# Final norm of the odd tiles on ScalarE and GpSimd instead of VectorE, and one semaphore for five products of the plan

## Chip, cores and metric

One core of one Trainium2 chip. The metric is the device time of one execution in microseconds (us), as a median over runs.

## What is computed

One step of a decoder layer: norm, input projection, convolution group and sparse attention group, output projection, residual, norm, a mixture of 32 gated experts (two per token), residual, and a last norm. Only the end of it matters here:

```python
def rmsnorm(x, g):
    xf = x.astype(jnp.float32)
    y = xf * lax.rsqrt(jnp.mean(xf * xf, axis=-1, keepdims=True) + RMS_EPS)
    return (y * g.astype(jnp.float32)).astype(x.dtype)
# the experts' results, weighted and summed per token, are added to x; then
# y = rmsnorm(x, ln_final), for 1024 prompt rows and 32 sample rows of D_MODEL = 1024
```

## The kernel before

The tokens are 1056 rows: eight tiles of 128 rows and a ninth (tile 8) of 32. All values are float32. The program is written as one stream per engine, with semaphores between them; an engine runs its stream strictly in the order written. `chain(ins)` makes an engine wait for its own instruction `ins`.

The last block of the kernel has two parts that the diff touches.

**The plan** (VectorE from L2312, TensorE from L2278). VectorE works out which expert takes which rows in which round. TensorE supplies five products in this order, each with a semaphore of its own: `counted`, `prefixed`, `experts_turned` (L2287), `table_made` (36 products at L2293), `small_doubled` (L2298). VectorE waits for them at L2326, L2354 (`experts_turned`), L2361 (`prefixed`), L2406 and L2411.

**The experts** follow: 17 rounds, each with one expert on 128 rows and one on up to 64, whose weights stream in through SyncE's queue while TensorE multiplies. GpSimd gathers rows and scatters results to `scratch_y` in device memory.

**The final stage** begins when the last results are in `scratch_y`. Four streams run it, each over the nine tiles in order:

- SyncE, `load_results` (L2229): for every tile two loads of 512 KB (the two experts' rows), into one of three places (YS = 3). The loads of tile t wait until the sums of tile t - 3 are done.
- VectorE, `sum_results`: in step t the two weighted sums of tile t (L2246, one SCALAR_TENSOR_TENSOR per expert), then, of tile t - 1, the reciprocal of the root (L2254) and one SCALAR_TENSOR_TENSOR that multiplies by it and by the gains `final_g` into `final` (L2257). `final` has two places, one for even tiles and one for odd ones; before L2257 of tile q, VectorE waits at L2256 until the store of tile q - 2 has landed (`final_out0`, `final_out1`).
- ScalarE, `result_moments`: Square with a sum over the row (L2265), then the root (L2267). It loads the table of the root first (L2261).
- GpSimd, `store_results`: waits for `final_ready` and issues the store of 512 KB (L2236). Tile 8 is 32 rows. At the end it waits until all stores have landed.

The lines of VectorE and GpSimd that the change replaces:

```python
if q >= 2:
    dve.wait_ge(sem(f"final_out{q % 2}"), 16 * (q // 2))
dve.scalar_tensor_tensor(final[:n, q % 2, :], x_res[:n, q, :], rs9[:n, q:q + 1],
                         final_g[:n, :], ALU.mult, ALU.mult).then_inc(sem("final_ready"), 1)
...
pool.wait_ge(sem("final_ready"), t + 1)
pool.dma_start(dst, final[:rows(t), t % 2, :]).then_inc(sem(f"final_out{t % 2}"), 16)
```

Earlier in the kernel, other lines serve as measures: L849 is GpSimd's addition of a bias to 128x512; L636 and L638 are its copies of 128x256; L542 and L545 are VectorE's taps of the convolution on 128x1024, a TENSOR_SCALAR and then SCALAR_TENSOR_TENSORs; L1679, L1681 and L1690 are ScalarE's Square, Sqrt and Copy in the stage of the second norm.

Of the kernel before, what the change touches and what calls it, by code (L numbers as in the profile page):

```python
# [24 lines left out]
ALU = mybir.AluOpType  # L25
# [113 lines left out]
def build(nc, a):  # L139

    _, const_at, const_small = const_table()
    with ExitStack() as ctx:
# [11 lines left out]
        def sem(name):  # L154

            if name not in semaphores:
                semaphores[name] = nc.alloc_semaphore(name)
            return semaphores[name]
# [2073 lines left out]
        def store_results(pool):  # L2232
            for t in range(TILES):
                pool.wait_ge(sem("final_ready"), t + 1)
                dst = out["out0"][P * t:P * t + P, :] if t < NQ else out["out1"]
                pool.dma_start(dst, final[:rows(t), t % 2, :]).then_inc(sem(f"final_out{t % 2}"), 16)  # L2236
            pool.wait_ge(sem("final_out0"), 16 * 5)
            pool.wait_ge(sem("final_out1"), 16 * 4)

        def sum_results(dve, chain):  # L2240
            for t in range(TILES + 1):
                if t < TILES:
                    n = rows(t)
                    dve.wait_ge(sem(f"y_rows_in{t % YS}"), 32 * (t // YS + 1))
                    for j, w in enumerate((first_w, second_w)):
                        ins = dve.scalar_tensor_tensor(x_res[:n, t, :], y_rows[:n, t % YS, j, :], w[:n, t:t + 1],  # L2246
                                                       x_res[:n, t, :], ALU.mult, ALU.add)
                        if j == 0:
                            chain(ins)
                    ins.then_inc(sem("rows_summed"), 1)  # L2250
                if t >= 1:
                    q, n = t - 1, rows(t - 1)
                    dve.wait_ge(sem("sd9_ready"), q + 1)
                    chain(dve.reciprocal(rs9[:n, q:q + 1], sd9[:n, q:q + 1]))  # L2254
                    if q >= 2:
                        dve.wait_ge(sem(f"final_out{q % 2}"), 16 * (q // 2))  # L2256
                    dve.scalar_tensor_tensor(final[:n, q % 2, :], x_res[:n, q, :], rs9[:n, q:q + 1],  # L2257
                                             final_g[:n, :], ALU.mult, ALU.mult).then_inc(sem("final_ready"), 1)

        def result_moments(act, chain):  # L2260
            chain(act.activation(table9, con("eps")[:, 0:1], ACT.Sqrt))  # L2261
            for t in range(TILES):
# [4 lines left out]
                act.activation(sd9[:n, t:t + 1], ms9[:n, t:t + 1], ACT.Sqrt, bias=con("eps")[:n, 0:1])\  # L2267
                   .then_inc(sem("sd9_ready"), 1)

        with nc.Block() as block:  # L2270
# [7 lines left out]
            def _(pe):  # L2278
                for name in ("upped0", "upped1", "downed0", "downed1", "xg_turned0", "xg_turned1"):
                    pe.sem_inc(sem(name), 1)  # L2280
                pe.matmul(ps[:, 1, 0:E_], con("ones"), counted_to[:, TILES], start=True, stop=True)\
                  .then_inc(sem("counted"), 1)
                pe.matmul(ps[:, 0, 0:288], con("before"), both.rearrange("p t n -> p (t n)"), start=True, stop=False)
                pe.matmul(ps[:, 0, 0:288], con("ones"), counted_to[:, 0:TILES].rearrange("p t n -> p (t n)"),
                          start=False, stop=True).then_inc(sem("prefixed"), 1)
                pe.wait_ge(sem("experts_set"), 1)
                pe.matmul(ps[0:1, 3, 0:COLS + 1], expert_f, ident[:, 0:COLS + 1], start=True, stop=True)\  # L2287
                  .then_inc(sem("experts_turned"), 1)
                for q in range(2 * TILES):
                    n = rows(q % TILES)  # L2290
                    if q % TILES == 0:
                        pe.wait_ge(sem("one_hots"), q // TILES + 1)
                    mm = pe.matmul(ps[:, 2, 0:COLS], one_slot[:n, q, :], one_chunk[:n, q, :],  # L2293
                                   start=(q == 0), stop=(q == 2 * TILES - 1))
                mm.then_inc(sem("table_made"), 1)
                pe.wait_ge(sem("small_table"), 1)
                for h in range(2):
                    mm = pe.matmul(ps[HF * h:HF * h + HF, 7, 0:ROUNDS], ident[:HF, :HF], small_table[:HF, :],  # L2298
                                   start=True, stop=True, tile_position=(0, HF * h))
                mm.then_inc(sem("small_doubled"), 1)  # L2300
                expert_products(pe)
# [11 lines left out]
            def _(dve):  # L2313
                chain = Chain(dve, sem("dve_chain"), count["dve"])

                def each(v):
# [8 lines left out]
                n_large, n_small = n_both[:, 0:E_], n_both[:, E_:2 * E_]  # L2325
                dve.wait_ge(sem("counted"), 1)  # L2326
                dve.tensor_scalar(n_large, ps[:, 1, 0:E_], -0.5, 1.0 / P, ALU.add, ALU.mult)
# [25 lines left out]
                                               ALU.subtract))  # L2353
                dve.wait_ge(sem("experts_turned"), 1)  # L2354
                dve.tensor_copy(row_ints[0:1, 0:2 * ROUNDS + 1], ps[0:1, 3, 0:COLS + 1]).then_inc(sem("plan_ready"), 1)
# [4 lines left out]
                chain(dve.tensor_scalar(shift, shift, float(ROUNDS), float(P), ALU.add, ALU.mult))  # L2360
                dve.wait_ge(sem("prefixed"), 1)  # L2361
                places = ps[:, 0, 0:288].rearrange("p (t n) -> p t n", n=E_)
# [42 lines left out]

                dve.wait_ge(sem("table_made"), 1)  # L2406
                large, small = ps[:, 2, 0:ROUNDS], ps[:, 7, 0:ROUNDS]
                dve.tensor_copy(small_table[:HF, :], ps[:HF, 2, ROUNDS:COLS]).then_inc(sem("small_table"), 1)
                tokens(LARGE, large)
                dve.tensor_copy(ints[:, 0:ROUNDS], rows_f[:, LARGE]).then_inc(sem("table_ready"), 1)  # L2410
                dve.wait_ge(sem("small_doubled"), 1)  # L2411
                tokens(SMALL, small)
# [93 lines left out]
```

## Time and profile before

| what | us |
|---|---|
| runs, median (lowest to highest of 3) | 1594.9 (1592.1 to 1597.46) |
| the profiled execution | 1597.91 |
| its span, first to last instruction | 1596.1 |
| TensorE busy (share of the span) | 1394.6 (87%) |
| VectorE busy | 673.3 (42%) |
| ScalarE busy | 370.8 (23%) |
| GpSimd busy | 215.4 (13%) |

The span is that of one execution under the profiler; the execution's own time has about 2 us around it. PE is TensorE's matmuls, PEld its weight loads, DVE is VectorE, ACT is ScalarE, POOL is GpSimd, SP is SyncE, and a q behind a name (POOLq) is the engine's sequencer or queue. L2257 is line 2257 of the kernel. "arena" is the one large tensor in SBUF of which nearly all tiles are parts, "ps" is PSUM. The final stage runs from about 1544 us to the end.

### The profile page before, as it was taken

The page shows a single profiled execution, that of the slowest core. Times are in us where ns is not written, and L with a number is a line of the kernel's source. Part 1 is how long each engine was busy: PE and PEld are TensorE (multiplying, and loading weights), DVE is VectorE, ACT ScalarE, POOL GpSimd, SP SyncE. Part 2 cuts the span into 40 slices and gives each one's busy share as a digit, 9 for nine tenths or more (in the row PEclk, how much of TensorE's full clock was granted, in tenths as well). Part 3 has the DMA queues.
Part 4 walks back from the last instruction along what each step waited for, and adds up shares of the span by engine and source line. Part 5 has one row for each costly group of instructions (what it writes and reads, how often), then busy time and mean ns, then how long its engine had stood idle before and what let it go on. Part 6 is the DMA issues. An engine that isn't in the chain of part 4 may idle for free. (4 is left out here: it accounts for less than half of the span.)

```text
span 1596.1 us, 22287 instructions
## 1 busy us (share of the span) xinstructions
PE 1394.6 (87%) x7454; PEld 824.0 (52%) x7454; DVE 673.3 (42%) x1413; ACT 370.8 (23%) x802; POOL 215.4 (13%) x379
## 2 busy tenths in 40 slices
PE   5999999849888988886999938999999999999950
PEld 3665544449755665554555524444544445544430
DVE  3398688541368777766244460101011001111027
ACT  4000011141156555544111101111111111111112
POOL 0000111184222000005000000111111111111111
PEclk8999999969769999997999958999999999999985
DMA  8500000096245000008512057999999999999935
GB/s 289 211 40 1 14 14 20 23 333 212 76 137 167 28 2 14 2 17 247 160 54 79 30 211 294 404 410 407 411 414 408 412 394 397 408 400 395 404 137 223
DMA packets 93623, 330.94 MB, mean 207 GB/s; under 512 B 12374, under 2 KB 52695, under 8 KB 70818
## 3 DMA queue, kind: packets, MB, share of 16 engines
q1 hardware_dynamic: 77082, 290.78, 46.7%
q0 software_dynamic: 16464, 39.19, 6.9%
q8 instruction: 41, 0.67, 0.2%
q14 instruction: 36, 0.29, 0.1%
HBM read 313.11 MB, written 31.62 MB: 216 GB/s over the span
## 5 line engine op out<-in xcount | busy, mean ns | idle before, releaser
L2085 PE MATMUL ps<-arena 128*128 128x512 f32 x544 | 238.5, 596 | 0.0
L2085 PEld LDWEIGHTS ps<-arena 128*128 128x128 f32 x544 | 102.2, 190 | 135.6 <-issue 135.6
L545 DVE SCALAR_TENSOR_TENSOR arena<-arena 128x1024 f32<-128x1024 f32 x120 | 147.5, 1281 | 1.2
L378 PE MATMUL ps<-arena 128*128 128x512 f32 (+1 forms) x384 | 141.2, 528 | 0.0
L2094 PE MATMUL ps<-arena 128*64 128x256 f32 x1088 | 121.2, 381 | 0.0
L332 PE MATMUL ps<-arena 128*128 128x352 f32 x384 | 117.3, 468 | 4.3 <-issue 3.8
L2138 PE MATMUL ps<-arena 128*128 128x512 f32 x272 | 119.5, 592 | 0.0
L1553 PE MATMUL ps<-arena 128*128 128x512 f32 x256 | 114.9, 603 | 0.6 <-ACT arena L1662 0.6
L1156 ACT ACTIVATE arena<-ps,arena 128x640 f32<-128x640 f32 (+7 forms) x128 | 89.8, 702 | 108.8 <-DVE arena L1232 103.8
L378 PEld LDWEIGHTS ps<-arena 128*128 128x128 f32 x384 | 72.5, 190 | 66.7 <-issue 61.2
L2198 DVE TENSOR_TENSOR arena<-arena,ps 128x512 f32<-128x512 f32 x17 | 11.7, 688 | 225.3 <-PE ps L2085 225.3
L1053 PE MATMUL ps<-arena 128*128 128x128 f32 x528 | 87.1, 289 | 20.8 <-DVE arena L1250 10.0
L2094 PEld LDWEIGHTS ps<-arena 128*64 128x64 f32 x1088 | 76.6, 137 | 49.7 <-issue 12.9
L332 PEld LDWEIGHTS ps<-arena 128*128 128x128 f32 x384 | 74.2, 194 | 46.0 <-issue 6.5
L1232 DVE TENSOR_REDUCE arena<-ps 128x1 f32<-128x640 f32 (+7 forms) x128 | 90.6, 708 | 4.4
L263 POOL DMA_DIRECT2D arena<-in_cache_sel x96 | 51.6, 537 | 300.1 <-POOLq L954 208.0
L724 PE MATMUL ps<-arena 128*128 128x128 f32 (+1 forms) x512 | 64.1, 290 | 20.5 <-DMA arena<-in_cache_cmp 19.9
L1067 PE MATMUL ps<-arena 128*64 128x128 f32 x1056 | 73.3, 282 | 9.4 <-ACT arena L1163 4.7
L1053 PEld LDWEIGHTS ps<-arena 128*128 128x128 f32 x528 | 57.2, 142 | 46.5 <-issue 19.0
L2138 PEld LDWEIGHTS ps<-arena 128*128 128x128 f32 x272 | 50.5, 191 | 56.9 <-issue 56.9
L1031 PE MATMUL ps<-arena 64*128 64x512 f32 (+3 forms) x384 | 76.8, 508 | 1.1 <-ACT arena L1143 0.7
L1553 PEld LDWEIGHTS ps<-arena 128*128 128x128 f32 x256 | 48.3, 194 | 56.2 <-issue 55.2
(365 smaller groups left out, 1575.1 us busy)
## 6 DMA issues: line engine op xcount, KB each, us to landing
arena<-in_w_gate SPq DMA_DIRECT2D x34, 2048.0 KB, 8.2
arena<-in_w_up SPq DMA_DIRECT2D x34, 2048.0 KB, 14.1
arena<-in_w_down SPq DMA_DIRECT2D x34, 2048.0 KB
arena<-in_x_prompt SPq DMA_DIRECT2D x16, 512.0 KB, 6.3
arena<-in_cache_cmp SPq DMA_DIRECT2D x64, 128.0 KB, 6.0
arena<-in_cache_cmp POOLq DMA_DIRECT2D x64, 128.0 KB, 5.6
arena<-in_cache_sel SPq DMA_DIRECT2D x64, 128.0 KB, 2.4
arena<-scratch_y SPq DMA_DIRECT2D x16, 512.0 KB, 5.9
```

The costliest lines, as they stand in the source:

```text
L332: mm = pe.matmul(ps[:, 4 + 2 * (u % 2) + half, 0:NW], w_conv[:, k, half * CH + c * P:half * CH + c * P + P], xT[:, k, j * NW:(j + 1) * NW] ...
L378: mm = pe.matmul(ps[:n, b + o // 512, 0:w], xT[:, k, t * P:t * P + n], w_tm[:, k, o:o + w], start=(k == 0), stop=(k == KT_ - 1))
L545: ins = dve.scalar_tensor_tensor(o, i, dw[:, c, j:j + 1], o, ALU.mult, ALU.add)
L1031: mm = pe.matmul(ps[:, score_bank(p, g) + o // 4, 0:n], qT[64 * g:64 * g + 64, r, i * P:(i + 1) * P], kT[64 * g:64 * g + 64, w, (first + o ...
L1053: mm = pe.transpose(ps[:, turn_bank("chunk", c), j * P:(j + 1) * P], probs_of(h, m)[:, (o + j) * P:(o + j + 1) * P], ident)
L1067: mm = pe.matmul(ps[64 * g:64 * g + 64, 6, r * P:(r + 1) * P], vals[:, first + j, w, 64 * g:64 * g + 64], pT[:, (2 * p + g) % 3, j * P:(j ...
L1156: act.activation(probs_of(h, m), scores(p, g), ACT.Exp, bias=neg_max[:, h % 4:h % 4 + 1], accum_out=sums[:, i % 2, w, R * g + r:R * g + r ...
L1232: dve.tensor_reduce(neg_max[:, h % 4:h % 4 + 1], s, AX.X, ALU.max, negate=True)\
L1553: mm = pe.matmul(ps[:n, 2 + half, :], mixT[:, t % 2, k, 0:n], w_out(k, 512 * half, 512), start=(k == 4), stop=(k == 3))
L2085: mm = pe.matmul(ps[:, bank, :], xgT_l[:, k, :], w[LARGE][:, k, :], start=(k == 0), stop=(k == KT_ - 1))
L2094: mm = pe.matmul(ps[HF * h:HF * h + HF, bank, 0:HH], xgT_s[:, q, HF * part:HF * part + HF], w[SMALL][:, k, HH * h:HH * h + HH], start=(k = ...
L2138: mm = pe.matmul(ps[:, half, :], hidT_l[:, q // 2, q % 2, :], w_down[LARGE][:, q // 2, q % 2, 512 * half:512 * half + 512], start=(q == 0) ...
```

## The change

The final stage treats odd and even tiles differently. For even tiles nothing changes but the index. For an odd tile q VectorE only computes the reciprocal and signals `final_scale`. ScalarE, once it has done the root of tile q + 1, waits for that signal and for the store of tile q - 2, and copies `x_res` of the tile into `final` with the reciprocal as its scale. GpSimd waits for the copy, multiplies by `final_g` in place, waits for its own product and issues the store. The five semaphores of the plan's products become one, `plan_product`, with targets 1 to 5.

```diff
@@ -2231,7 +2231,13 @@
 
         def store_results(pool):
             for t in range(TILES):
-                pool.wait_ge(sem("final_ready"), t + 1)
+                if t % 2:
+
+                    pool.wait_ge(sem("odd_scaled"), t // 2 + 1)
+                    pool.tensor_tensor(final[:, 1, :], final[:, 1, :], final_g, ALU.mult).then_inc(sem("odd_final"), 1)
+                    pool.wait_ge(sem("odd_final"), t // 2 + 1)
+                else:
+                    pool.wait_ge(sem("final_ready"), t // 2 + 1)
                 dst = out["out0"][P * t:P * t + P, :] if t < NQ else out["out1"]
                 pool.dma_start(dst, final[:rows(t), t % 2, :]).then_inc(sem(f"final_out{t % 2}"), 16)
             pool.wait_ge(sem("final_out0"), 16 * 5)
@@ -2251,11 +2257,15 @@
                 if t >= 1:
                     q, n = t - 1, rows(t - 1)
                     dve.wait_ge(sem("sd9_ready"), q + 1)
-                    chain(dve.reciprocal(rs9[:n, q:q + 1], sd9[:n, q:q + 1]))
-                    if q >= 2:
-                        dve.wait_ge(sem(f"final_out{q % 2}"), 16 * (q // 2))
-                    dve.scalar_tensor_tensor(final[:n, q % 2, :], x_res[:n, q, :], rs9[:n, q:q + 1],
-                                             final_g[:n, :], ALU.mult, ALU.mult).then_inc(sem("final_ready"), 1)
+                    ins = dve.reciprocal(rs9[:n, q:q + 1], sd9[:n, q:q + 1])
+                    if q % 2:
+                        ins.then_inc(sem("final_scale"), 1)
+                    else:
+                        chain(ins)
+                        if q >= 2:
+                            dve.wait_ge(sem("final_out0"), 16 * (q // 2))
+                        dve.scalar_tensor_tensor(final[:n, 0, :], x_res[:n, q, :], rs9[:n, q:q + 1],
+                                                 final_g[:n, :], ALU.mult, ALU.mult).then_inc(sem("final_ready"), 1)
 
         def result_moments(act, chain):
             chain(act.activation(table9, con("eps")[:, 0:1], ACT.Sqrt))
@@ -2266,6 +2276,15 @@
                                      accum_out=ms9[:n, t:t + 1]))
                 act.activation(sd9[:n, t:t + 1], ms9[:n, t:t + 1], ACT.Sqrt, bias=con("eps")[:n, 0:1])\
                    .then_inc(sem("sd9_ready"), 1)
+                if t % 2 == 0 and t > 0:
+                    scale_odd(act, t - 1)
+
+        def scale_odd(act, t):
+            act.wait_ge(sem("final_scale"), t // 2 + 1)
+            if t >= 3:
+                act.wait_ge(sem("final_out1"), 16 * (t // 2))
+            act.activation(final[:, 1, :], x_res[:, t, :], ACT.Copy, scale=rs9[:, t:t + 1])\
+               .then_inc(sem("odd_scaled"), 1)
 
         with nc.Block() as block:
             @block.sync
@@ -2279,25 +2298,25 @@
                 for name in ("upped0", "upped1", "downed0", "downed1", "xg_turned0", "xg_turned1"):
                     pe.sem_inc(sem(name), 1)
                 pe.matmul(ps[:, 1, 0:E_], con("ones"), counted_to[:, TILES], start=True, stop=True)\
-                  .then_inc(sem("counted"), 1)
+                  .then_inc(sem("plan_product"), 1)
                 pe.matmul(ps[:, 0, 0:288], con("before"), both.rearrange("p t n -> p (t n)"), start=True, stop=False)
                 pe.matmul(ps[:, 0, 0:288], con("ones"), counted_to[:, 0:TILES].rearrange("p t n -> p (t n)"),
-                          start=False, stop=True).then_inc(sem("prefixed"), 1)
+                          start=False, stop=True).then_inc(sem("plan_product"), 1)
                 pe.wait_ge(sem("experts_set"), 1)
                 pe.matmul(ps[0:1, 3, 0:COLS + 1], expert_f, ident[:, 0:COLS + 1], start=True, stop=True)\
-                  .then_inc(sem("experts_turned"), 1)
+                  .then_inc(sem("plan_product"), 1)
                 for q in range(2 * TILES):
                     n = rows(q % TILES)
                     if q % TILES == 0:
                         pe.wait_ge(sem("one_hots"), q // TILES + 1)
                     mm = pe.matmul(ps[:, 2, 0:COLS], one_slot[:n, q, :], one_chunk[:n, q, :],
                                    start=(q == 0), stop=(q == 2 * TILES - 1))
-                mm.then_inc(sem("table_made"), 1)
+                mm.then_inc(sem("plan_product"), 1)
                 pe.wait_ge(sem("small_table"), 1)
                 for h in range(2):
                     mm = pe.matmul(ps[HF * h:HF * h + HF, 7, 0:ROUNDS], ident[:HF, :HF], small_table[:HF, :],
                                    start=True, stop=True, tile_position=(0, HF * h))
-                mm.then_inc(sem("small_doubled"), 1)
+                mm.then_inc(sem("plan_product"), 1)
                 expert_products(pe)
 
             @block.scalar
@@ -2323,7 +2342,7 @@
 
 
                 n_large, n_small = n_both[:, 0:E_], n_both[:, E_:2 * E_]
-                dve.wait_ge(sem("counted"), 1)
+                dve.wait_ge(sem("plan_product"), 1)
                 dve.tensor_scalar(n_large, ps[:, 1, 0:E_], -0.5, 1.0 / P, ALU.add, ALU.mult)
                 chain(dve.tensor_scalar(n_small, ps[:, 1, 0:E_], 63.5, 1.0 / P, ALU.add, ALU.mult))
                 chain(dve.tensor_scalar(n_both, n_both, ROUNDING, None, ALU.add))
@@ -2351,14 +2370,14 @@
                 chain(dve.scalar_tensor_tensor(large_at, cum[:, 0:E_], float(P), large_rows, ALU.mult, ALU.subtract))
                 chain(dve.scalar_tensor_tensor(small_at, cum[:, E_:2 * E_], all_large, n_small, ALU.subtract,
                                                ALU.subtract))
-                dve.wait_ge(sem("experts_turned"), 1)
+                dve.wait_ge(sem("plan_product"), 3)
                 dve.tensor_copy(row_ints[0:1, 0:2 * ROUNDS + 1], ps[0:1, 3, 0:COLS + 1]).then_inc(sem("plan_ready"), 1)
                 chain(dve.tensor_scalar(excess, rounds_f, all_large, float(ROUNDS), ALU.subtract, ALU.add))
                 chain(dve.tensor_scalar(spill, small_at, rounds_f, excess, ALU.is_ge, ALU.mult))
                 chain(dve.tensor_tensor(small_at, small_at, spill, ALU.subtract))
                 chain(dve.tensor_tensor(shift, small_at, cum[:, 0:E_], ALU.subtract))
                 chain(dve.tensor_scalar(shift, shift, float(ROUNDS), float(P), ALU.add, ALU.mult))
-                dve.wait_ge(sem("prefixed"), 1)
+                dve.wait_ge(sem("plan_product"), 2)
                 places = ps[:, 0, 0:288].rearrange("p (t n) -> p t n", n=E_)
                 dve.tensor_tensor(slot, places, each(large_at), ALU.add)
                 chain(dve.tensor_tensor(late, places, each(large_rows), ALU.is_ge))
@@ -2403,12 +2422,12 @@
                     chain(dve.scalar_tensor_tensor(rows_f[:, s], rows_, -1.0, second_half[:, s], ALU.add, ALU.subtract))
                     chain(dve.scalar_tensor_tensor(rows_f[:, s], rows_f[:, s], 0.0, empty[:, s], ALU.max, ALU.add))
 
-                dve.wait_ge(sem("table_made"), 1)
+                dve.wait_ge(sem("plan_product"), 4)
                 large, small = ps[:, 2, 0:ROUNDS], ps[:, 7, 0:ROUNDS]
                 dve.tensor_copy(small_table[:HF, :], ps[:HF, 2, ROUNDS:COLS]).then_inc(sem("small_table"), 1)
                 tokens(LARGE, large)
                 dve.tensor_copy(ints[:, 0:ROUNDS], rows_f[:, LARGE]).then_inc(sem("table_ready"), 1)
-                dve.wait_ge(sem("small_doubled"), 1)
+                dve.wait_ge(sem("plan_product"), 5)
                 tokens(SMALL, small)
                 dve.tensor_scalar(ints[:, ROUNDS:2 * ROUNDS], rows_f[:, SMALL], 2.0, con("upper"), ALU.mult, ALU.add)\
                    .then_inc(sem("table_ready"), 1)
```

## Rows read from the trace of the kernel before

**Rows 1.** The page, part 4: shares of the chain that ended last
```profile
PE 36%; DMA 2%; DVE 2%; issue 0%; ACT 0%; POOL 0%; POOLq 0%; SPq 0%; DVEq 0%
PE ps L2085 15%; PE ps L2094 8%; PE ps L2138 7%; PE ps L2147 4%; PE ps L2074 1%; DMA out<-arena 1%; PE ps L2124 1%; DVE arena L2246 1%; DMA arena<-scratch_h,ints 1%; PE ps L2293 1%; PE ps L2080 1%; DVE arena L2257 0%; DMA scratch_y<-arena,ints 0%; DMA arena<-scratch_y 0%; PE ps L2130 0%
```

**Rows 2.** The final stage in two windows; start:end, then busy us (count) by engine
```profile
core 0: us, PE busy (x) PEld busy (x) DVE busy (x) ACT busy (x) POOL busy (x), PEclk, DMA share, GB/s
1549.00:1573.00 24.00, 0.00 (x0) 0.00 (x0) 21.63 (x22) 8.64 (x18) 2.22 (x4) 0.50 1.00 376
1573.00:1587.00 14.00, 0.00 (x0) 0.00 (x0) 13.10 (x15) 4.36 (x10) 2.34 (x5) 0.50 0.42 171
```

**Rows 3.** Timeline of the final stage, parts; start us, us, engine, line
```profile
1558.48 1.28 DVE L2257 SCALAR_TENSOR_TENSOR arena<-arena 128x1024 f32<-128x1024 f32 x1
...
1559.68 2.60 DVE L2246 SCALAR_TENSOR_TENSOR arena<-arena 128x1024 f32<-128x1024 f32 x2
1560.06 0.56 POOL L2236 DMA_DIRECT2D out<-arena  x1 [3.31 <-DVE arena L2257]
...
1562.60 1.29 DVE L2257 SCALAR_TENSOR_TENSOR arena<-arena 128x1024 f32<-128x1024 f32 x1 [0.24 <-DMA out<-arena]
...
1571.90 1.29 DVE L2257 SCALAR_TENSOR_TENSOR arena<-arena 128x1024 f32<-128x1024 f32 x1 [0.32 <-DMA out<-arena]
...
1580.92 2.57 DVE L2246 SCALAR_TENSOR_TENSOR arena<-arena 32x1024 f32<-32x1024 f32 x2
...
1583.53 1.06 ACT L2265 ACTIVATE arena<-arena 32x1024 f32<-32x1024 f32 x1 [2.41 <-DVE arena L2246]
...
1584.71 0.30 ACT L2267 ACTIVATE arena<-arena 32x1 f32<-32x1 f32 x1
...
1585.22 1.27 DVE L2257 SCALAR_TENSOR_TENSOR arena<-arena 32x1024 f32<-32x1024 f32 x1
1586.79 0.52 POOL L2236 DMA_DIRECT2D out<-arena  x1 [1.07 <-DVE arena L2257]
```

**Rows 4.** Waits of the final stage; total us, times, longest
```profile
DVE arena L2257 <- DMA out<-arena: 1.8, 3, 1.2
```

**Rows 5.** Stores of L2236 issued from 1556 to 1570: time to landing
```profile
DMA to landing us min/median/max: 6.0/7.0/7.6
```

**Rows 6.** The same, issued from 1573 to 1586
```profile
DMA to landing us min/median/max: 2.9/2.9/3.8
```

**Rows 7.** The same, the last store, issued at 1586.8
```profile
DMA to landing us min/median/max: 2.2/2.2/2.2
```

**Rows 8.** GpSimd's only multiply or add of long rows, line 849
```profile
L849 POOL TENSOR_TENSOR arena<-arena x9: 1255/1262/1275, 343.6 to 353.4; 128x512 f32<-128x512 f32 x8, 32x512 f32<-32x512 f32 x1
```

**Rows 9.** ScalarE by line, 700 to 960 us: count, busy us, mean ns
```profile
L1679 ACT ACTIVATE arena<-arena 128x1024 f32<-128x1024 f32 (+1 forms) x9 | 9.5, 1057 | 57.4 <-DVE arena L1832 55.7 <-DVE arena L1847 1.7
...
L1690 ACT ACTIVATE arena<-ps 128x512 f32<-128x512 f32 (+1 forms) x9 | 5.0, 559 | 9.1 <-PE ps L1572 9.1
...
L1681 ACT ACT_TABLE_LOAD x1 | 1.3, 1283 | 0.0
```

**Rows 10.** Where GpSimd and VectorE met: timeline, then lines 638 and 545
```profile
166.88 1.78 DVE L542 TENSOR_SCALAR arena<-arena 128x1024 f32<-128x1024 f32 x2
...
168.05 0.86 POOL L638 COPY arena<-arena 128x256 f32<-128x256 f32 x1
...
168.58 1.41 DVE L545 SCALAR_TENSOR_TENSOR arena<-arena 128x1024 f32<-128x1024 f32 x1
...
L638 POOL COPY arena<-arena x8: 409/409/861, 168.1 to 307.8; 128x256 f32<-128x256 f32 x8
...
L545 DVE SCALAR_TENSOR_TENSOR arena<-arena x120: 1272/1279/1411, 72.0 to 296.7; 128x1024 f32<-128x1024 f32 x120
```

**Rows 11.** Timeline of the plan: VectorE's wait for the table
```profile
951.22 0.18 DVE L2408 COPY arena<-ps 64x32 f32<-64x32 f32 x1 [2.87 <-PE ps L2293]
```

**Rows 12.** Loads of L2229 issued from 1551 to 1568: time to landing
```profile
DMA to landing us min/median/max: 4.1/5.9/8.6
```

## The prediction

> **What bounds the kernel now.** I start at the chain that ended last [rows 1]. It is a chain of matmul lines; the two lines of the final stage, L2246 (the weighted sums) and L2257 (scaling by the root and by the gains), hold 1% each or less. So the change can move only the last 3% of the span, and I leave the first 1549 us alone. The window view of that stage [rows 2] splits it in two. From 1549 to 1573 us the DMA share is 1.00 and VectorE is busy 21.63 of 24.00 us: both are full, so what VectorE gives up there may be lost to transfers. From 1573 to 1587 us the DMA share is 0.42 and VectorE is busy 13.10 of 14.00 us: there VectorE alone sets the pace. The timeline [rows 3] gives the period of a tile when nothing disturbs it: two sums 2.60, a reciprocal, one L2257 of 1.28, about 3.9 us. It also gives the tail: the sums of the last tile begin at 1580.92 and end at 1583.49, Square starts at 1583.53, the root ends at 1585.01, L2257 runs at 1585.22, and the last store is issued at 1586.79 and lands 2.2 us later [rows 7], at 1589.0. The remaining 7.1 us to the end of the span (1596.1) follow the last landing and move with it. Last, VectorE waits for stores only 1.8 us in all [rows 4], though stores land 6.0 to 7.6 us after issue in the full part [rows 5] and 2.9 to 3.8 us after it later [rows 6].
>
> **The change, part by part.**
>
> The plan's semaphores. Five become one with targets 1 to 5. TensorE signals in program order, and each wait asks for the product it asked for before; the wait for 3 was, on an engine that finishes in order, already a wait for the two before it. The one wait I see there, 2.87 us for the table [rows 11], stays. Cost 0.
>
> VectorE loses L2257 for tiles 1, 3, 5 and 7: 4 x 1.28 = 5.1 us. It also loses the wait for store 1 in front of tile 3's L2257, most of the 1.8 us; that in front of tile 2's (1562.60) stays.
>
> ScalarE gains four copies of 128x1024. Square at the same shape takes 1.057 us [rows 9]; I take 1.06. Copy, Square and Sqrt already alternate over nine tiles at L1690, L1679 and L1681, and the loads of tables there are one [rows 9], so no reload. Copy q comes after the root of tile q+1, so nothing of the next even tile is behind it, but the Square of tile q+2 is.
>
> GpSimd gains four multiplies of 128x1024. The only row of its kind is 128x512 at 1.262 us, nine of them back to back from 343.6 to 353.4, so 1.225 each [rows 8]. Twice that is 2.45; with all of its time a fixed cost it would be 1.26, twice the single duration is 2.52. I take 2.45, since what is per element should double. GpSimd waits for each product before it issues the store, and the store of the next even tile stands behind that in its queue. An odd tile now needs copy 1.06 + multiply 2.45 + about 0.3 to the issue = 3.8 us before its transfer, against 1.28 + 0.3; and it cannot start until ScalarE has done the next tile's root, 1.5 us after its sums.
>
> Do VectorE and GpSimd disturb each other? Nothing in the final stage shows it, but one place earlier does [rows 10]. GpSimd's copy takes 0.409 alone and 0.861 beside VectorE's TENSOR_SCALAR; it gets through only about where that ends (166.88 + 1.78 = 168.66), and the SCALAR_TENSOR_TENSOR that starts there (168.58) takes 1.41 instead of 1.279 while the copy finishes by 168.91. They seem to take turns at reading. **I take it that a multiply on GpSimd holds back a SCALAR_TENSOR_TENSOR for as long as it runs, and the reverse.** The low end is that they do not touch each other; between them lies a proportion, 0.13 lost of 0.33 overlapped. I choose the first because a two-input multiply reads nearly all its time, where a short copy reads for part of it.
>
> The Trainium skill (SBUF — State Buffer, section "Who interferes with whom") states that a VectorE instruction with two SBUF inputs contends with a GpSimd instruction that reads SBUF, and that the first to start keeps the pair for its whole length. By that rule the overlap of 0.33 would have cost 0.33, and the row shows 0.13; for this kernel the rule in full gives the forecast below, its denial gives the first rival.
>
> **The walk with turns.** Until 1558.45 nothing differs. Tile 3's sums go 1558.5 to 1561.1 (1.2 early; their rows are there, since loads land 4.1 to 8.6 us after issue [rows 12] and this one was issued at 1551.9). Copy 1 at 1560.0 to 1561.1, multiply 1 to 1563.6, store 1 at 1563.9 (was 1560.06, +3.8). L2257 of tile 2 was ready at 1562.6 and waits for the multiply: 1563.6 to 1564.9. Tile 4's sums to 1567.5 (+1.1), tile 5's to 1570.2 (1.3 early). Store 1 lands at about 1569 to 1570, so copy 3 runs to about 1570.1 and multiply 3 to 1572.6; store 2, issued at 1565.2 behind store 1 in one queue, lands at about 1572 (1565.2 + 6.4). L2257 of tile 4 therefore goes 1572.6 to 1573.9 (was 1571.90): the 1.3 us won are gone. Tile 6's sums to 1576.5 (+0.8), tile 7's to 1579.2 (-0.4). Copy 5 to 1579.2, multiply 5 to 1581.7, L2257 of tile 6 behind it to 1583.0, tile 8's sums to 1585.6 (was 1583.49, +2.1). Tail: root of tile 8 at 1587.1, copy 7 to 1588.2, L2257 of tile 8 to 1588.6, multiply 7 to 1591.05, store 7 at 1591.35, landing 2.9 later at 1594.3; store 8 right behind lands by then too. Against 1589.0 that is **+5.3 us**. In short: VectorE gives up 5.1 and 1.8 of old waits, gets 9.0 back as waits for multiplies and late stores (so tile 8's sums end 2.1 later), and the tail grows from 5.5 to 8.7.
>
> The profiled execution took 1597.9 around its span of 1596.1, 3.0 above the median of the three runs. So 1603.2 for that execution, and 1594.9 + 5.3 = 1600.2 for the median. About 0.3% (4.8 us) is what a measurement of this kernel can tell from no change.
>
> **Rivals.**
> 1. They do not disturb each other (30%). For it: the overlap row is one place and small. L2257 of tile 2 stays at 1562.6; tile 4's waits for store 2, now about 1571.5; tile 6's sums to 1575.4, tile 7's to 1578.0, L2257 of tile 6 to 1579.4, tile 8's sums to 1582.0 (1.5 early). Then the longer tail: root 1583.5, copy 7 waits for store 5 (issued 1580.8) to 1583.7 and ends at 1584.8, multiply to 1587.3, store 7 lands 1590.5: +1.5, or 1596.4. Its own range is 0 to +3.5; the proportion of [rows 10] gives about +3. All of that is within 0.3%.
> 2. VectorE's relief arrives in full (5%): late stores are never waited for, since fewer transfers collide. Tile 8's sums end 5.1 + 1.8 early, the tail costs 3.2 more: -3.7, or 1591.2. Against it stands the DMA share of 1.00. It passes 0.3% only if the multiply is nearer 1.26.
> 3. The odd ring is the bound (12%): copy 1.06, multiply, store 7.6 is one buffer's round, since copy 3 waits for store 1. With a multiply of 2.45 the round is 11.4 us against two tiles at 7.8. VectorE would not see it, but ScalarE would: copy 3 stands in front of Square 5, and copy 5 in front of Square 7. If each of three rounds costs 1.5 beyond the forecast, or the multiply is starved by VectorE's back-to-back sums, +9 to +10: 1604.5. It decides where the multiply exceeds some 3.5 us.
> 4. The odd tiles are not really moved, or the table is reloaded, 2 x 1.28 per odd tile: 1% (the diff shows the first, [rows 9] speaks against the second).
>
> The forecast has 52%, its own range is +3.5 to +7.5 (1598.4 to 1602.4). Slower by over 0.3%: 0.6 of the forecast's 52% plus rival 3, 0.43. Faster by over 0.3%: part of rival 2, 0.04. Same: 0.53. The range reaches down to most of rival 1 and up to the forecast's upper end and part of rival 3: 1594.5 to 1604.
>
> **What would show it.** Right: L2257 five times instead of nine; GpSimd with TENSOR_TENSOR 128x1024 four times at 2.45; SCALAR_TENSOR_TENSOR or the multiply longer than 1.29 or 2.5 wherever they overlap, or L2257 and the sums starting only at a multiply's end; VectorE waiting 1 us or more for store 2; the last two stores issued within 1 us of each other, both behind a multiply. Wrong: all VectorE durations at 1.28 beside a running multiply (rival 1); ScalarE's Square of tiles 5 and 7 late by more than 1.5 us (rival 3); tile 8's sums ending before 1582 (rival 1 or 2); anything before 1549 us moved.

## The result and the profile after

The changed kernel takes 1598.7 us (median of 20 runs) against 1594.0 for the kernel before in the same runs: ratio 1.0028, 95% interval 1.0021 to 1.0036. That is 4.5 us slower (0.0028 x 1594). The prediction was 1600.2 against 1594.9, +5.3.

The profiled execution spans 1598.3 us (1596.1 before). Its final stage begins 4.2 us earlier, though: the first load is issued at 1540.30 us, against 1544.50 before. The code ahead of it differs only by the name of a semaphore, and over the traces of this study that point lies anywhere from 1538.6 to 1544.6. So I compare the stage by itself, from its first load to the end of the span: 51.6 us before, 58.0 after.

Busy time by line in the final stage (count, busy us, mean ns, then idle time before and what ended it), first of the kernel before:

```profile
L2246 DVE SCALAR_TENSOR_TENSOR arena<-arena 128x1024 f32<-128x1024 f32 (+1 forms) x18 | 23.0, 1281 | 9.1 <-DMA arena<-scratch_y 8.8
L2257 DVE SCALAR_TENSOR_TENSOR arena<-arena 128x1024 f32<-128x1024 f32 (+1 forms) x9 | 11.6, 1284 | 2.0 <-DMA out<-arena 1.8
```

then of the changed kernel, where the sums are L2252, the gains of the even tiles L2267, ScalarE's copy L2286, GpSimd's multiply L2237 and its stores L2242:

```profile
L2252 DVE SCALAR_TENSOR_TENSOR arena<-arena 128x1024 f32<-128x1024 f32 (+1 forms) x18 | 25.1, 1396 | 9.8 <-DMA arena<-scratch_y 9.5
L2237 POOL TENSOR_TENSOR arena<-arena 128x1024 f32<-128x1024 f32 x4 | 10.6, 2643 | 18.1 <-ACT arena L2286 18.1
L2267 DVE SCALAR_TENSOR_TENSOR arena<-arena 128x1024 f32<-128x1024 f32 (+1 forms) x5 | 10.0, 2001 | 2.1 <-DMA out<-arena 2.1
...
L2286 ACT ACTIVATE arena<-arena 128x1024 f32<-128x1024 f32 x4 | 4.6, 1140 | 1.4 <-DMA out<-arena 1.4
```

The line of the gains ran nine times and now runs five times, but VectorE's time in it went only from 11.6 to 10.0 us, and the 18 sums went from 23.0 to 25.1. Four instructions fewer, and VectorE is busy as long as before. The timeline shows where (start, length, engine, line):

```profile
1557.59 2.34 POOL L2237 TENSOR_TENSOR arena<-arena 128x1024 f32<-128x1024 f32 x1 [4.27 <-ACT arena L2286]
1558.28 2.73 DVE L2267 SCALAR_TENSOR_TENSOR arena<-arena 128x1024 f32<-128x1024 f32 x1 [0.67 <-DMA out<-arena]
...
1566.09 1.15 ACT L2286 ACTIVATE arena<-arena 128x1024 f32<-128x1024 f32 x1 [1.04 <-DMA out<-arena]
...
1567.15 1.28 DVE L2267 SCALAR_TENSOR_TENSOR arena<-arena 128x1024 f32<-128x1024 f32 x1 [0.97 <-DMA out<-arena]
1567.32 3.32 POOL L2237 TENSOR_TENSOR arena<-arena 128x1024 f32<-128x1024 f32 x1 [5.46 <-ACT arena L2286]
...
1568.36 4.68 DVE L2252 SCALAR_TENSOR_TENSOR arena<-arena 128x1024 f32<-128x1024 f32 x2
...
1576.16 3.43 DVE L2267 SCALAR_TENSOR_TENSOR arena<-arena 128x1024 f32<-128x1024 f32 x1 [0.43 <-DMA out<-arena]
1576.17 2.34 POOL L2237 TENSOR_TENSOR arena<-arena 128x1024 f32<-128x1024 f32 x1 [4.11 <-ACT arena L2286]
...
1583.50 1.13 ACT L2286 ACTIVATE arena<-arena 128x1024 f32<-128x1024 f32 x1
...
1583.81 1.27 DVE L2267 SCALAR_TENSOR_TENSOR arena<-arena 32x1024 f32<-32x1024 f32 x1
1584.72 2.57 POOL L2237 TENSOR_TENSOR arena<-arena 128x1024 f32<-128x1024 f32 x1 [4.29 <-ACT arena L2286]
1587.59 1.11 POOL L2242 DMA_DIRECT2D out<-arena  x2 [0.30 <-POOL arena L2237]
```

I call an instruction held when it takes longer because the other engine's runs. A VectorE instruction that starts inside a multiply, or beside its start, ends about 1.1 us after it, nearly its own length: 2.73, 3.36 (the first of the pair of 4.68) and 3.43 us where 1.28 is usual, 5.7 us in all (5.0 in the second trace of this kernel, below). The reverse is there too: at 1567.32 L2267 was already running, and the multiply takes 3.32. So it is for the last multiply: it starts 0.36 us before tile 8's L2267 ends and takes 2.57 instead of 2.34. That multiply is on the way to the end, and the last two stores leave together behind it; in the kernel before they left 1.6 us apart, the last at 1586.79 [rows 3].

### The profile page after: what moved, and what is told of

Its sections match the earlier page's. It is cut to its first block and busy times, and to the rows that moved or that the text cites. A ratio compares the mean times of both kernels' runs of the same rounds, so it can differ in the third digit from the quotient of the medians.

```text
span 1598.3 us, 22291 instructions
## 1 busy us (share of the span) xinstructions
PE 1394.6 (87%) x7454; PEld 824.1 (52%) x7454; DVE 673.8 (42%) x1409; ACT 374.7 (23%) x806; POOL 225.2 (14%) x383
```

## Experiments

All ratios are against the kernel before, in the same runs, with 95% intervals. "Body" is from the first load of the final stage to the end of tile 8's sums, "tail" from there to the end of the span, both in us and read from each run's one trace.

| kernel | ratio | body | tail | stage |
|---|---|---|---|---|
| before | | 39.0 | 12.6 | 51.6 |
| changed | 1.0028 (1.0021 to 1.0036) | 41.8 | 16.2 | 58.0 |
| plan's semaphores only | 0.9991 (0.9976 to 1.0005) | 40.4 | 12.6 | 53.0 |
| changed, no multiply | 0.9984 (0.9970 to 0.9997) | 38.4 | 13.5 | 51.9 |
| before + four multiplies beside | 1.0032 (1.0017 to 1.0046) | 43.3 | 14.4 | 57.7 |
| before + four memsets beside | 1.0013 (0.9997 to 1.0028) | 39.6 | 13.6 | 53.2 |
| changed, tile 7 back | 1.0018 (1.0007 to 1.0029) | 41.1 | 12.6 | 53.7 |
| changed, only tile 7 | 1.0044 (1.0029 to 1.0058) | 38.8 | 16.2 | 55.0 |
| changed, three places | 1.0035 (1.0022 to 1.0048) | 40.7 | 16.3 | 57.1 |
| before, stores by SyncE | 0.9947 (0.9932 to 0.9962) | 37.7 | 5.4 | 43.1 |
| changed, gains in PSUM | 1.0027 (1.0011 to 1.0042) | 38.4 | 16.0 | 54.4 |
| changed, stores by SyncE, one tile later | 1.0048 (1.0028 to 1.0068) | 45.6 | 11.4 | 57.0 |
| changed, again | 1.0029 (1.0017 to 1.0042) | 40.2 | 16.2 | 56.5 |
| changed, only tile 7, again | 1.0019 (1.0008 to 1.0029) | 39.9 | 16.2 | 56.1 |

The same code differs by up to 1.6 us in the body from trace to trace (39.0 and 40.4; 41.8 and 40.2), so a difference of one trace's body below that shows nothing; the tail repeats within 0.1.

### Is it the semaphores?

```diff
-dve.wait_ge(sem("counted"), 1)            # and four others alike
+dve.wait_ge(sem("plan_product"), 1)
```

> The kernel before with only the plan's five semaphores made one; the final stage untouched. Both theories (the cost is VectorE and GpSimd taking turns; the cost is the longer way of an odd tile) expect 0 against the kernel before, within 1.5 us, and every duration of the final stage as before. A difference of 3 us or more would put part of the change's +4.5 us here.

Measured 0.9991, interval 0.9976 to 1.0005: no difference, so the effect is in the final stage.

### Is it the multiply?

```diff
 pool.wait_ge(sem("odd_scaled"), t // 2 + 1)
-pool.tensor_tensor(final[:, 1, :], final[:, 1, :], final_g, ALU.mult).then_inc(sem("odd_final"), 1)
-pool.wait_ge(sem("odd_final"), t // 2 + 1)
```

> The changed kernel without GpSimd's multiply: ScalarE's copy goes straight to the store, so the odd tiles lack the gains. Theory of turns: every SCALAR_TENSOR_TENSOR is back at 1.27 to 1.29 us; beside the 2.9 us of the tail (2.57 and 0.3) the 1.3 + 2.1 + 2.1 us that VectorE was held come back too, partly as waits for stores: 5 to 8 us faster than the changed kernel, that is 0.5 to 3.5 us faster than the kernel before. Rival, the longer way of an odd tile alone: only the tail's 2.9 us come back, 1.5 us slower than the kernel before.

Measured 0.9984, 2.5 us faster than before and so 7 us faster than the changed kernel, inside what the theory of turns expected and outside the rival. VectorE is back at its lengths:

```profile
L2250 DVE SCALAR_TENSOR_TENSOR arena<-arena 128x1024 f32<-128x1024 f32 (+1 forms) x18 | 23.0, 1280 | 10.5 <-DMA arena<-scratch_y 10.2
L2265 DVE SCALAR_TENSOR_TENSOR arena<-arena 128x1024 f32<-128x1024 f32 (+1 forms) x5 | 6.4, 1282 | 3.8 <-DMA out<-arena 3.7
```

VectorE gave up 5.2 us (29.4 against 34.6), but its waits for stores rose from 1.8 [rows 4] to 3.7 and for loads by 1.4 (10.2 against 8.8): where the DMA share is 1.00 [rows 2], relief of VectorE turns into waits for transfers. Even with a multiply that cost nothing, four instructions of 1.28 would have bought about 2.5 us by the timed runs (0.5 to 4.8 by their interval); the stage of this one trace, 51.9, is only 0.4 us below the mean of the two with the stage of before.

### Does a multiply hold VectorE when nobody waits for it, and a memset not?

To the kernel before (with the one semaphore of the plan), after the store of each odd tile:

```diff
+if t % 2:
+    pool.tensor_tensor(spare9, final_g, final_g, ALU.mult).then_inc(sem("spare_made"), 1)
+    pool.wait_ge(sem("spare_made"), t // 2 + 1)
```

and in the other kernel `pool.memset(spare9w, 0.0)` over 128x2048 in that place.

> The kernel before (with the plan's one semaphore) plus four multiplies of 128x1024 on GpSimd, each after the store of tiles 1, 3, 5 and 7, of the gains by themselves into an unused tile; nobody waits for the result. Theory of turns: VectorE is held about 2.3 us by each; at tiles 1 and 3 part of it vanishes in transfers, at tiles 5 and 7 it counts in full: 5 to 9 us slower than the kernel before, with four SCALAR_TENSOR_TENSORs of 2.5 to 3.6 us. Rival: no engine waits for these multiplies, so 0 to +1 us and all at 1.28.

> The same four places, with a memset of 128x2048 on GpSimd instead of the multiply: it only writes. If the turns are about reading, as the theory has it, VectorE's SCALAR_TENSOR_TENSORs stay at 1.27 to 1.29 us and the time is that of the kernel before, within 1.5 us. If any GpSimd instruction of that length holds VectorE (or the store behind it in the queue is what costs), it comes out slower by 3 us or more like the run with multiplies.

With multiplies 1.0032, +5 us; with memsets 1.0013, +2 us, an interval that reaches below 1. The sums of each kernel (min/median/max ns), first with the multiplies:

```profile
L2251 DVE SCALAR_TENSOR_TENSOR arena<-arena x18: 1266/1284/2796, 1545.7 to 1582.9; 128x1024 f32<-128x1024 f32 x16, 32x1024 f32<-32x1024 f32 x2
```

and, with the memsets, the sums and the memsets themselves:

```profile
L2251 DVE SCALAR_TENSOR_TENSOR arena<-arena x18: 1266/1284/1286, 1545.3 to 1578.8; 128x1024 f32<-128x1024 f32 x16, 32x1024 f32<-32x1024 f32 x2
...
L2240 POOL MEMSET arena<- x4: 1823/1823/1824, 1557.0 to 1582.3; 128x2048 f32 x4
```

Three sums of 2.80 us beside the multiplies, where I had expected four held instructions, and none over 1.286 beside memsets of 1.82. At the fourth multiply VectorE was first, and the multiply is the one held, 2.52 us where the other three take 2.07 to 2.10:

```profile
1585.92 1.27 DVE L2262 SCALAR_TENSOR_TENSOR arena<-arena 32x1024 f32<-32x1024 f32 x1
1586.44 2.52 POOL L2240 TENSOR_TENSOR arena<-arena 128x1024 f32<-128x1024 f32 x1
```

A busy GpSimd alone does not hold VectorE: the multiply, which reads SBUF, does, and the memset, which only writes, does not. Both tails grew (14.4 and 13.6 against 12.6): the fourth extra instruction stands between the last two stores in GpSimd's queue, which is about 1 of the 2 us of the memsets, where at most 1.5 had been expected; the rest is within the interval. The body with the multiplies is 2.9 to 4.3 us longer than that of before; +5 us is the lower end of what was expected.

### What is the tail worth?

The changed kernel with a list of the tiles that are moved, (1, 3, 5) in one and (7,) in the other:

```diff
-if t % 2:
+if t in MOVED:
```

> The changed kernel with tile 7 back on VectorE: only tiles 1, 3 and 5 go through ScalarE and GpSimd. If the tail is a term of its own (16.2 us from the end of tile 8's sums to the end of the span in the changed kernel, 12.6 before), these 3.6 us come back and the held VectorE remains: about +1 to +2.5 us against the kernel before, and the sums of tile 8 end as late as in the changed kernel. Rival, the turns are all of it: no more than 1 us comes back, +3.5 us or more.

> The changed kernel with only tile 7 moved; tiles 1, 3 and 5 on VectorE as before. Theory with a tail term: tile 8's sums end where they did before, and the way root, copy, multiply, store of tile 7 makes the tail 3 to 3.6 us longer: +2.5 to +4 us against the kernel before. Rival, the turns are all of it: the multiply of tile 7 meets only the last, idle VectorE, so 0 to +1 us.

> Only tile 7 moved, a second time, since +7 us was more than its own profile shows: there the stage is 55.0 us, 2 to 3.4 over the stage of before. If the profile is right, +2.5 to +5 us; if the first figure is, +6 us or more, and then the start of the stage, not the stage, must be later.

With tile 7 back: 1.0018, +2.9 us, just above the expected band, tail 12.6 again and body 41.1, as late as in the changed kernel. With tile 7 alone the first run gave 1.0044 (6 runs), more than expected; the second gave 1.0019 (11 runs, +3.0 us), in the band. The intervals only touch, at 1.0029, so one of them may be off by more than its interval says; both profiles agree that the tail is 16.2 and the body that of the kernel before (38.8 and 39.9). I take the tail as +3.6 us and leave open what the first figure held. In both traces with tile 7 alone no SCALAR_TENSOR_TENSOR is over 1.29 us, so VectorE is never held, and all that turns add is the 0.2 us by which tile 8's L2267 holds the multiply (2.57 us): the rival "turns are all of it" falls.

### Are the late stores a term?

```diff
-final = flat(A1 + YS * 2048, 2048).rearrange("p (s n) -> p s n", s=2)
+final = flat(A1 + YS * 2048, 3072).rearrange("p (s n) -> p s n", s=3)   # places t % 3, waits for tile t - 3
```

> The changed kernel with three places for finished tiles instead of two, so a copy or L2267 waits for the store of three tiles ago. It takes away the waits for late stores (ScalarE 1.4 us, VectorE 2.1 us in the changed kernel) but leaves every multiply. If late stores are a term, 1 to 3 us faster than the changed kernel, +1.5 to +3.5 us against the kernel before; if only turns and tail count, within 1 us of the changed kernel, +3.5 to +5.5 us.

Measured 1.0035, +5.6 us, just over the changed kernel's own +3.5 to +5.5. No engine waits for a store any more in its trace, and it is not faster than the changed kernel: of the two outcomes expected, the one in which late stores are no term of their own. Without these waits VectorE meets all three multiplies head on:

```profile
1570.82 2.34 POOL L2237 TENSOR_TENSOR arena<-arena 128x1024 f32<-128x1024 f32 x1 [4.31 <-ACT arena L2286]
1570.92 3.32 DVE L2267 SCALAR_TENSOR_TENSOR arena<-arena 128x1024 f32<-128x1024 f32 x1
```

L2267 took 3.37, 3.32 and 3.37 us in it, 6.2 us lost against 5.7 in the changed kernel.

### Is it the second input from SBUF?

```diff
 chain(act.activation(table9, con("eps")[:, 0:1], ACT.Sqrt))
+for b in range(2):
+    chain(act.activation(ps[:, 3 + b, :], final_g[:, 512 * b:512 * b + 512], ACT.Copy))
...
-                         final_g[:n, :], ALU.mult, ALU.mult)
+                         gains_ps[:n, :], ALU.mult, ALU.mult)
```

> The changed kernel with the gains copied to PSUM once by ScalarE, before its first Square, and read from there by VectorE's L2267 (GpSimd still reads them from SBUF). The sums keep their two SBUF inputs. If VectorE is held because both its inputs come from SBUF, no L2267 is longer than 1.35 us even beside a running multiply, and only the sum behind it is held, by what is left of the multiply (about 1.1 us instead of 2.1): 1 to 4 us faster than the changed kernel. If any VectorE instruction is held by a multiply, L2267 of 2.7 to 3.4 us stay and the time is the changed kernel's within 1 us.

L2267 now reads one operand from PSUM and is never held, also where it runs wholly beside a multiply; the sum behind it, with both inputs in SBUF, is:

```profile
1572.27 2.35 POOL L2237 TENSOR_TENSOR arena<-arena 128x1024 f32<-128x1024 f32 x1 [3.88 <-ACT arena L2290]
1572.32 1.28 DVE L2267 SCALAR_TENSOR_TENSOR arena<-arena,ps 128x1024 f32<-128x1024 f32 x1
...
1573.52 3.48 DVE L2252 SCALAR_TENSOR_TENSOR arena<-arena 32x1024 f32<-32x1024 f32 x2
...
1579.38 1.27 DVE L2267 SCALAR_TENSOR_TENSOR arena<-arena,ps 32x1024 f32<-32x1024 f32 x1 [0.69 <-DMA out<-arena]
1579.63 2.34 POOL L2237 TENSOR_TENSOR arena<-arena 128x1024 f32<-128x1024 f32 x1 [3.59 <-ACT arena L2290]
...
L2267 DVE SCALAR_TENSOR_TENSOR arena<-arena,ps x5: 1267/1279/1281, 1548.8 to 1579.4; 128x1024 f32<-128x1024 f32 x4, 32x1024 f32<-32x1024 f32 x1
its engine sat idle before it (us, times) until:
  DMA out<-arena: 4.7, 3
```

So the mechanism is as expected, to the end of the multiply. The reverse goes too: the last multiply takes 2.34 us although tile 8's L2267 runs for its first 1.0 us, where it took 2.57 beside an L2267 with both inputs in SBUF. The expected gain of 1 to 4 us was not shown: 1.0027, beside 1.0029 for the changed kernel in the same runs, with intervals too wide to exclude 2 us. VectorE's held time fell from 5.7 to about 1.0 us, its waits for stores rose from 2.1 to 4.7. The stage of this one trace is 2.1 to 3.6 us shorter.

### Who holds the end of the program?

In each trace so far GpSimd's closing DRAIN of 6.68 us begins just after the last store has landed. The kernel before, with

```diff
-    pool.wait_ge(sem("final_ready"), t + 1)      # GpSimd: and its dma_start, and the final waits
+    sp.wait_ge(sem("final_ready"), t + 1)        # SyncE: store of tile t - 4 behind the loads of tile t
```

> The kernel before with the nine stores issued and waited for by SyncE, behind its loads, instead of by GpSimd. In every trace so far GpSimd's closing DRAIN of 6.68 us begins only when its last store has landed, and the span ends right after it. If that drain only needs GpSimd to be finished, it now runs beside the final stage and 5 to 7 us go: 0.9955 to 0.997 of the kernel before. Rival: something at the program's end waits as long for the last landing whoever issued it, so within 1 us of the kernel before.

Measured 0.9947 (0.9932 to 0.9962), 8.5 us faster than the kernel before, more than the 5 to 7 expected: the fastest kernel here. The drain rows, first of the kernel before:

```profile
L2270 POOLq DRAIN  x1: 6677/6677/6677, 1589.2 to 1589.2; - x1
```

then of this one, where it runs at the start of the stage beside everything else:

```profile
L2273 POOLq DRAIN  x1: 5942/5942/5942, 1544.9 to 1544.9; - x1
...
L2273 SPq DRAIN  x1: 13/13/13, 1583.9 to 1583.9; - x1
```

The tail falls from 12.6 to 5.4 us, 7.2 of the 8.5; the body is 1.3 to 2.7 us shorter too, with 0.4 us of waits for stores in place of 1.8. Stores by SyncE in the changed kernel leave GpSimd its multiplies. The edit is not quite the same: here the store of tile t - 5 stands behind the loads of tile t, above it was tile t - 4.

> The changed kernel with the stores issued by SyncE, as in the run with stores by SyncE, so GpSimd only multiplies. If GpSimd's closing DRAIN of 6.7 us starts when GpSimd's own work is over, it starts at the end of tile 7's multiply, near the end of the stage, and nearly all of what stores by SyncE gave (about 8 us) is lost again: 3 to 5 us faster than the changed kernel, 0 to +2 us against the kernel before. If the gain came from SyncE's faster stores instead, it should stay: 6 to 9 us faster than the changed kernel.

```profile
L2295 POOLq DRAIN  x1: 8580/8580/8580, 1588.6 to 1588.6; - x1
```

This drain starts beside tile 7's multiply (1588.62 to 1591.20) and ends 5.97 us after it, at 1597.17, though the last store had landed by 1594.4. The gain is lost, as expected; that the kernel is not even faster than the changed one (1.0048 against 1.0029, overlapping intervals) was not expected. In its trace VectorE waits 9.3 us for stores, and the body is 45.6 us. The timeline shows where the wait comes from:

```profile
1551.36 4.70 SPq L2229 DMA_DIRECT2D arena<-scratch_y  x4
...
1551.44 1.28 DVE L2273 SCALAR_TENSOR_TENSOR arena<-arena 128x1024 f32<-128x1024 f32 x1
...
1552.64 2.60 DVE L2258 SCALAR_TENSOR_TENSOR arena<-arena 128x1024 f32<-128x1024 f32 x2
...
1556.11 0.43 SPq L2244 DMA_DIRECT2D out<-arena  x1
...
1562.47 1.28 DVE L2273 SCALAR_TENSOR_TENSOR arena<-arena 128x1024 f32<-128x1024 f32 x1 [4.58 <-DMA out<-arena]
```

Tile 0 was finished at 1552.7, but its store stands in SyncE's stream behind the loads of tile 5, which wait for tile 2's sums (to 1555.2). It is issued at 1556.11, 3.4 us after the tile was ready, and L2273 of tile 2, which needs its place, waits 4.58 us. The same happens with store 2 (issued 1567.15) and L2273 of tile 4, 4.72 us. In the kernel before with stores by SyncE, store 0 was issued at 1552.35, as soon as its tile was ready. So this run says where the drain stands, by its rows; its time is also that of stores queued one tile later, and it is no clean price for the multiplies. With t - 4 it was not run.

### The control

> The changed kernel itself, as a control beside the others and for a second profile of its final stage. +3.5 to +5.5 us against the kernel before; from the first load of the final stage to the end of the span 56.5 to 58.5 us (58.0 in the first profile; 51.6 and 53.0 in the two with the stage of before).

1.0029, +4.6 us, and stage 56.5 us, the lower end: both as expected.

## Why the prediction was right

**The sign, the size and the mechanism held.** +4.5 us measured, +5.3 forecast; the means of the two traces of each final stage give 57.2 against 52.3, +4.9. The ratio, 1.0028, is just under the 0.3% that I called the bound, so by that bound the outcome was "same", which had 0.53; its interval excludes no change.

**The plan's semaphores**: 0, as said (0.9991).

**The walk.** Shifted by the 4.2 us that the stage began earlier, its times come out as follows, forecast first: multiply 1 at 1561.1, was 1561.8; store 1 at 1563.9, was 1564.4; tile 5's sums to 1570.2, was 1570.3; tile 7's to 1579.2, was 1579.9; tile 8's sums to 1585.6, was 1586.3; store 7 at 1591.35, was 1591.8; last landing 1594.3, was 1595.4 (issued at 1588.17, 3.1 to landing, + 4.2). So this pair of traces shows +6.4 where +5.3 stood. One order was wrong: I had L2257 of tile 4 wait for multiply 3, but store 2 landed first, L2267 ran, the multiply was held by it (3.32 us), and then tile 6's sum by the multiply (3.36 us). Multiply 3 ended at 1574.8 and not at 1572.6, because copy 3 came 1.3 us later than forecast and the multiply was held 1.0; yet tile 6's sums end only 0.7 us late (1577.2 for 1576.5), since VectorE did an instruction while the multiply waited. That the late multiply and the wrong order nearly cancel is in part luck.

**VectorE and GpSimd take turns.** I chose full turns over the proportion of [rows 10], and the rows bear that out: an instruction of 1.28 becomes 2.73 to 3.43 and ends 1.08 us after the multiply. That is 0.2 us less than its full length after it, so a multiply holds VectorE for all but its last 0.2 us, which would also fit the 0.13 lost of 0.33 that I had read as a proportion. The memsets show that a GpSimd instruction that only writes does not hold VectorE, the gains in PSUM that a VectorE instruction with one of its two long inputs in PSUM is not held. The rule of the Trainium skill (SBUF — State Buffer, section "Who interferes with whom") states both conditions, and these traces agree, for a SCALAR_TENSOR_TENSOR against a TENSOR_TENSOR. The section calls the shared ports an exclusive lock, and its words "for the whole instruction" stand in the sentence on VectorE's two-port modes; I carried them over to this pair, and there these traces show all but 0.2 us. Rival 1, no disturbance, falls.

**The single prices**: the multiply 2.34 for 2.45, and 2.57 at the end, where tile 8's L2267 holds it, which the walk did not have; the copy 1.13 to 1.15 for 1.06.

**The tail**: +3.2 forecast, +3.6 measured (16.2 against 12.6). The step that was short is the last landing: I had store 8 land together with store 7, 2.9 us after store 7's issue, but it is issued 0.6 us behind it and takes 3.1, so the last landing comes 3.6 us after that issue.

**VectorE's relief.** I had 5.1 and 1.8 us come back as 9.0 of waits. The walk is right there and this sum is not: tile 7's L2257 stands behind tile 8's sums, where it ran while ScalarE did tile 8's Square (1583.61 against 1583.53 us), so only three instructions, 3.8 us, could shorten the body, and 7.7 us is what had to come back for the walk's +2.1. The first trace has 8.5: 5.7 held, 2.1 of waits for stores, 0.7 more of waits for loads; less the 3.8 and the old 1.8 that makes +2.9, and the body of that trace is 2.8 longer. Over the traces the body is +1.3 (mean of two) to +2.8 (first pair) against +2.1 forecast.

Taken apart by the kernel without multiply: moving the work gives the body 1.3 us and costs the tail 0.9; the multiplies cost the body 2.6 and the tail 2.7. The two figures of the body rest on one trace of that kernel and are no surer than the 1.6 us by which bodies differ. So more than half of the loss is in the tail, where turns are 0.2 us, and I had shared it out rightly (2.1 and 3.2).

**Rival 3**, the odd ring as the bound, falls: with three places no copy waits for a store and nothing is won. **Rival 2**, full relief, falls by the +4.5 us themselves (its own gain was 1.3 us too large for the same reason); without the multiply 3.3 of the 5.2 us that VectorE gave up came back as waits. **Rival 4** falls too: L2267 ran five times, and no table was loaded in the stage. One of my signs of being wrong did come, something before 1549 us moved (the start of the stage, by 4.2 us); the run with only the plan's semaphores and the spread of that start over all traces say that it is not the change.

## What to carry to other kernels

Before VectorE work goes to GpSimd, ask what VectorE does meanwhile: here it ran instructions with two SBUF inputs back to back, and three multiplies of 2.34 us on GpSimd came back as 5.0 and 5.7 us of held VectorE time in two traces, for 5.1 saved, of which only 3.8 stood on the way to the end. Price the last item by its own way to the end: a slower route for tile 7 cost 3.6 us whatever it spared in the middle. And look at what follows the last landing: GpSimd's closing work was 6.7 us of the span, and giving the stores to an engine that closes quickly won more (8.5 us) than the change could have, as long as GpSimd had nothing else to do at the end.

## What was not expected of the hardware

- GpSimd's closing DRAIN takes 6.68 us after its last store and 5.97 us after its last multiply, against 0.007 to 0.13 us on SyncE; it starts when GpSimd's program ends, so it hides if GpSimd finishes early (5.94 us at 1544.9). The DRAINs with which GpSimd closes the four earlier blocks of the kernel before take 1.9 to 9.2 us.
- A ScalarE copy with a scale per partition takes 1.13 to 1.15 us for 128x1024, where Square takes 1.057.
- A multiply on GpSimd took 2.34 us, and 2.07 to 2.10 where both its inputs were the same tile. Where a SCALAR_TENSOR_TENSOR with both inputs in SBUF was already running, the multiply of the changed kernel ended 2.21 us after that instruction: it lost all of the overlap but 0.13 us (0.36 us of overlap made 2.57, 1.11 made 3.32).
- Which engine is first is not quite what the recorded starts say: VectorE was held where its instruction was recorded 0.01 us before the multiply (1576.16) and, with tile 7 back, 0.04 us before, but not at 0.17 us (1567.15).
- The point where the final stage begins varies by 6 us (1538.6 to 1544.6) between executions of the same code ahead of it, so a stage must be compared by its own length. Why it varies was not tried.
